# Mirrored odd heads, another order of grams and corner products, and gated weight splits in the chunk stage of a two-block model

## The reference

```python
proj = h @ w_in
pool_u, pool_g, q, k, v, ret_g, rw, rw_g, gate_logits = jnp.split(proj, points, axis=-1)
...
o_pool = causal_pool_mixer(pool_u, pool_w, pool_scale) * jax.nn.silu(pool_g)
...
def step(S, inp):
    r_t, w_t, k_t, v_t, a_t, b_t = inp
    sa = jnp.einsum('bhvk,bhk->bhv', S, a_t)
    S = (S * w_t[:, :, None, :] + sa[..., None] * b_t[:, :, None, :]
         + v_t[..., None] * k_t[:, :, None, :])
    return S, jnp.einsum('bhvk,bhk->bhv', S, r_t)

_, y = lax.scan(step, jnp.zeros((B, H, N, N), jnp.float32), xs)
```

## Time and profile before

| what | value |
|---|---|
| median of 3 runs | 1835.55 us (1833.15 to 1838.32) |
| the profiled execution | 1840.28 us, span 1838.2 us |
| granted PE clock, mean share of full speed | 0.968 |
| PE busy | 1718.2 us, 93% |
| PE weight loads busy | 1373.8 us, 75% |
| DVE busy | 1036.0 us, 56% |
| ACT busy | 800.7 us, 44% |
| POOL busy | 632.0 us, 34% |

### The profile page before, as it was taken

The page is one execution under the profiler, slowest core; times in us unless marked ns, Lnnn a source line. Parts: engine busy times, 40 slices in busy tenths (PEclk is TensorE's granted clock), DMA queues, the critical chain, the costliest instruction groups (busy, mean ns, idle before and its releaser), DMA issues. The chain is left out here.

```text
span 1838.2 us, 26011 instructions
## 1 busy us (share of the span) xinstructions
PE 1718.2 (93%) x10688; PEld 1373.8 (75%) x10688; DVE 1036.0 (56%) x1367; ACT 800.7 (44%) x1200; POOL 632.0 (34%) x344
## 2 busy tenths in 40 slices
PE   8999989999999899899999999989999999987783
PEld 6877778888888787688888888868888986544441
DVE  4346744666665325584556766443116627866675
ACT  2455522333223335542333222344337736866673
POOL 1336612424444434751243444433421021322210
PEclk7999989999999899998999999989999999999997
DMA  8223321215444323322122544333420067999994
GB/s 344 81 92 106 90 77 36 92 58 192 171 166 171 126 92 96 96 85 77 54 85 66 209 175 169 138 126 126 149 92 1 1 240 265 382 388 395 389 392 178
DMA packets 82605, 287.97 MB, mean 157 GB/s; under 512 B 30473, under 2 KB 30601, under 8 KB 65332
## 3 DMA queue, kind: packets, MB, share of 16 engines
q1 hardware_dynamic: 76708, 275.87, 41.6%
q0 software_dynamic: 5040, 8.25, 1.4%
q10 hardware_dynamic: 736, 2.14, 0.3%
HBM read 274.50 MB, written 22.61 MB: 162 GB/s over the span
## 5 line engine op out<-in xcount | busy, mean ns | idle before, releaser
L1525 POOL TENSOR_TENSOR wmem_r<-wmem,wmem_r 128x1024 fp32r<-128x1024 f32 x170 | 420.2, 2473 | 696.4 <-ACT wmem_r L1041 685.5
L721 PE MATMUL banks<-h_hi_r,wmem_r 128*128 128x512 f32 x1632 | 511.2, 392 | 6.9 <-POOL wmem_r L1525 6.9
L721 PEld LDWEIGHTS banks<-h_hi_r,wmem_r 128*128 128x128 f32 x1632 | 307.9, 189 | 77.0 <-POOL wmem_r L1525 9.4
L1041 ACT ACTIVATE wmem_r<-wmem 128x1024 fp32r<-128x1024 f32 x170 | 180.2, 1060 | 405.2 <-DMA wmem<-wstream 402.2
L721 PE MATMUL banks<-hT_r,wmem_r 128*128 128x512 f32 x816 | 319.0, 391 | 0.0
L721 PEld LDWEIGHTS banks<-hT_r,wmem_r 128*128 128x128 f32 x816 | 154.0, 189 | 31.3
L2725 DVE TENSOR_TENSOR slots_r<-slots,wmem_r 128x1024 fp32r<-128x1024 f32 x102 | 121.9, 1217 | 57.7 <-ACT wmem_r L2418 52.1
L2806 POOL TENSOR_TENSOR wmem_r<-wmem,wmem_r 128x1024 fp32r<-128x1024 f32 x30 | 74.8, 2493 | 202.3 <-ACT wmem_r L2276 202.3
L992 PE MATMUL banks<-slots_r,wmem_r 128*128 128x512 f32 x512 | 127.7, 389 | 0.0
L1465 DVE SCALAR_TENSOR_TENSOR ztp<-xT,c_act,ztp 128x256 f32<-128x256 f32 x168 | 122.8, 731 | 6.0
L741 PE MATMUL banks<-wmem_r,h_hi_r 128*128 128x512 f32 x384 | 118.9, 391 | 0.0
(11 more groups left out here) (450 smaller groups left out, 3043.1 us busy)
## 6 DMA issues: line engine op xcount, KB each, us to landing
wmem<-wstream SPq DMA_DIRECT2D x206, 512.0 KB, 3.3
slots<-experts SPq DMA_DIRECT2D x80, 1024.0 KB, 24.5
xT<-ada SPq DMA_DIRECT2D x24, 1024.0 KB, 5.8
xT<-experts SPq DMA_DIRECT2D x16, 1024.0 KB, 25.0
slots<-ada SPq DMA_DIRECT2D x8, 1024.0 KB, 18.0
x_keep<-xT SPq DMA_DIRECT2D x2, 2048.0 KB, 17.4
xT<-x_keep SPq DMA_DIRECT2D x2, 2048.0 KB, 8.1
dil_rows<-dil_once SPq DMA_DIRECT2D x1, 2560.0 KB
```

The lines of the kernel that those rows point to most:

```text
L721: mm = nc.tensor.matmul(o, r(lhs[:, k, :]), r(rhs[:, k, :]), start=(k == 0 and i == 0), stop=(k == KD - 1 and i == 2))
L1041: inc(nc.scalar.activation(r(chunk(b)[0]), w, ACT.Copy), "w_high")
L1525: inc(g.tensor_tensor(r(lo), lo, r(hi), ALU.subtract), "w_split")
```

## The change

Five things are changed, in both layers.

1. The list of jobs and PE's order: the diagonal grams come after the first gate projection instead of after the fourth, `bs` after the second, `tv` and `tb` after the third, and `tk` after the fourth. Only two of the first three grams stand ahead of the corner products; the third stands between `zp` and `zc`. ACT and SP follow this order, and ACT takes the three exponentials ahead of its copy of the first gate.
2. DVE takes all cumulative sums first, and the two products that need the key norms after them.
3. The sides depend on the head kind too: `v_side(m, e)` is `side_of[(m + e) % 2]`. In every product of a step the heads with `e` = 0 and `e` = 1 now use different halves of the partitions or of the output, and PE's loops take `e` inside `c`, so the two alternate. The transpositions are made by 64x64 pieces.
4. In a step ACT copies w of `e` = 0 and u of `e` = 1, and DVE copies w of `e` = 1 and u of `e` = 0. The last quarter of a gram is issued after the state's part of y, and the banks stand in another order.
5. POOL's splits in the chunk steps wait until the state of step 1, 3 or 5 is ready (`s_ready` 2, 4, 6), and its copies wait for an earlier split. The copies are made per head kind.

```diff
-        v_side = lambda m: side_of[m % 2]
-        u_side = lambda m: side_of[(m + 1) % 2]
+        v_side = lambda m, e: side_of[(m + e) % 2]
+        u_side = lambda m, e: side_of[(m + e + 1) % 2]
...
             project("pu")
-            project("pg")
-            after("rk_ready")
...
+            feature_job("pg0", FIRST["pg"])
             after("ar_ready", 1)
             after("bk_ready", 1)
             for x in range(NT // 2):
...
+            feature_job("pg1", FIRST["pg"] + 1)
+            after("rk_ready")
...
+            feature_job("pg2", FIRST["pg"] + 2)
...
+            for n in range(0, NT, 2):
+                token_rows("v", n, V_, v_side)
+            for n in range(0, NT, 2):
+                token_rows("b", n, A_, u_side)
+            feature_job("pg3", FIRST["pg"] + 3)
...
+            for m in range(GRAMS_FIRST - 1):
+                gram(m, gram_banks(m), range(CW))
             after("inv_spread")
             after("corner_ready")
             corner_products("zp", lambda at, i: zt[at, i, SUB:STEP], lambda at, i: tt[at, i, :], 1)
+            gram(GRAMS_FIRST - 1, gram_banks(GRAMS_FIRST - 1), range(CW))
             corner_products("zc", lambda at, i: tt[at, i, :], lambda at, i: zt[at, i, SUB:STEP], 0)
...
+                o_u = [open_bank(f"u{m}{e}") for e in range(2)]
+                more = m + GRAMS_FIRST < STEPS
+                if more:
+                    o_g = gram_banks(m + GRAMS_FIRST)
+                    gram(m + GRAMS_FIRST, o_g, range(CW - 1))
+
+                after("w_ready0", m + 1)
+                after("w_ready1", m + 1)
...
+                for c in range(CW):
+                    for e in range(2):
+                        mm = nc.tensor.matmul(o_u[e][u_side(m, e), heads[c]], zt[u_side(m, e), RW_H * (m // 2) + 2 * c + e, :],
...
+                if more:
+                    gram(m + GRAMS_FIRST, o_g, range(CW - 1, CW))
+                after("u_ready0", m + 1)
+                after("u_ready1", m + 1)
...
             for m in range(STEPS):
+                inc(v.tensor_copy(w_sb[u_side(m, 1), CW * RW_D:2 * CW * RW_D], bank(f"w{m}1")[u_side(m, 1), 0:CW * RW_D]), "w_ready1")
+                o = bank(f"u{m}0")[u_side(m, 0), 0:CW * RW_D].rearrange("p (c f) -> p c f", c=CW)
+                inc(v.tensor_copy(per_head(uv_of(m)[u_side(m, 0)])[:, 0], o), "u_ready0")
                 if m + GRAMS_FIRST < STEPS:
                     gram_mask(m + GRAMS_FIRST, 0)
...
+                after("v_copied", 2 * n + 2)
                 if n > 0:
+                    after("s_ready", 2 * n)
                     low(FIRST["retq"] + n - 1, FIRST["retq"] + n)
```

282 lines of the change are left out of this document (153 added, 129 removed).

## The result

The changed kernel takes 1823.62 us (median of 6 runs, 1819.75 to 1826.51) against 1837.09 us (6 runs, 1833.15 to 1839.87): ratio 0.9930, 95% interval 0.9918 to 0.9943. The gain is 13.5 us where 28.5 were forecast. The profiled execution took 1819.75 us, span 1818.0. Its stretches are those of the earlier trace rows, with two more for the grams and corner products: up to `rg`, `rg` to the first gram, grams and corner products, chunk steps, for each layer.

A forecast was written before the change was run, and what follows sets the result against it. PE was taken as the bound, busy 93% of the span, mostly with work in the chunk steps. 26.1 + 10.6 - 10.0 + 1.8 = 28.5 us gained, from a median of 1835.55 to 1807 us; range 1796 to 1825.

The forecast's parts named there:

- Step A: Chunk steps: w, y and u alternate halves, so periods fall from 5.70 to 4.35 or 4.0 us; 26.1 us gained.
- the row of s: Chunk steps: profile row where s alternates output halves and the next batch starts 0.52 us later; 0.55 taken for w, y.
- Without a gram ... they cost about 0.15 each: Steps 5 to 7, without a gram: the waits for the copies of w and u cost about 0.15 us each.
- I cost it at nothing: Chunk steps: POOL's gating of its three 2.4 us splits, due only when `retq` starts, was given no cost.
- Step B: Corner products: the waits for the inverse and the low clock go, 4.3 us taken per layer; 10.6 us gained.
- At full clock 256 records at the pace of the diagonal grams ... are 4.15 us: Corner products: 256 records 16 ns apart, the pace of 128 diagonal gram records in 2.10 us, take 4.15 us.
- With them I expect the low clock to go too: Corner products: with the waits of 2.63 and 1.87 us for the inverse, the half clock was to go.
- Step C: From the first gate to `rg`: a wait before the diagonal grams and half clock, 44.5 us per layer; 10.0 us lost.
- Step D: `rg`/`tg` projections: the waits of 0.82 and 1.01 us for splits of weights go; 1.8 us gained.
- the clock stays low: Rival, chance 0.14: small matmuls hold the clock down in the corner products and first step of each layer; 1816 us.
- the 10 us at 0.50: Sign of being wrong: a chunk stage that still has 10 us at half clock.
- PE starves before the diagonal grams: Rival, chance 0.07 (0.04 slower): POOL holds two products 4.4 us, half clock lasts; 10.4 us lost per layer, 1828 us.

The follow-up runs named there:

- control: The changed kernel once more, unedited: 1823.24 us, ratio 0.9927.
- spread2: Changed kernel, diagonal grams after the second gate, two ACT high parts later, v, b, k tokens each behind a projection, POOL's first `rg` split earlier: 1814.86 us.
- no_alternation: Changed kernel with the loops of w, u and y issuing all tiles of the first head kind before the second, mirrored layout kept: 1831.99 us.
- copies_undone: Changed kernel with both copies of w on ACT and both copies of u on DVE, as before: 1834.34 us.
- pool_ungated: Changed kernel without POOL's gates: its `retq` splits don't wait for the state, its copies of v not for splits: 1837.06 us.
- dummy32: Changed kernel with 32 more small matmuls in the wait before the diagonal grams: 1820.65 us.
- dummy64: Changed kernel with 64 more small matmuls in the wait before the diagonal grams: 1820.59 us.
- warm8: Changed kernel with seven matmuls of 128x512 in the wait before the diagonal grams: 1817.84 us.
- early_undone: Changed kernel with gates, bonus, diagonal grams and tokens again in the order of before: 1822.29 us.
- double_zc: Changed kernel with each matmul of the last corner products `zc` issued twice in a row: 1830.46 us.

## Why the prediction was wrong

The sum went into the right direction, and each mechanism was at work, but the gain is less than half. From the sums of squares to `retq` the two traces of the changed kernel (changed, control) are 18.0 and 15.6 us shorter than before, where 28.5 were summed.

*Step A, 26.1 forecast, 20.2 and 20.8 measured.* The mirrored halves overlap as the row of s said, and a step with a gram takes 4.24 us (4.35). Two terms failed. "Without a gram ... they cost about 0.15 each": PE waits 0.76 us for the copy of w and 0.27 for that of u, and the period is 4.35 instead of 4.0. The copy itself takes 0.42; the two hand-overs, PE to DVE and back, take the other 0.34, and I had counted 0.1. And step 0 up to s takes 4.44 and 4.64 us instead of 3.0. Its wait for ACT's last corner copies, 0.75 and 0.94 us, was in the sum with 0.6; what was not is the half clock, on which both layers start the steps (252.88 to 256.29, 833.15 to 839.98). spread2, whose second layer has the same wait and full clock, takes 3.68. Three periods by 0.35 and 1.44 for step 0, less four by 0.11, are 2.1 us: the first layer's 35.07 against 33.0. The second layer's 3.9 us over 33.0 are the same and the longer low clock: its first period is 5.32 us instead of 4.20.

*Its reading of the cause was too narrow.* Alternation alone gives 4.3 and 3.2 us per layer (no_alternation), the divided copies 5.5 and 4.7 (copies_undone), POOL's gate 7.6 and 6.7 (pool_ungated). These do not add, since each was measured with the other two in place. "I cost it at nothing" was wrong of the gate as a part of the change: the sum with a scaling of 0.46 us holds only because of it.

*Step B, 10.6 forecast, 6.2 and 3.0 measured.* The failed step is "At full clock 256 records at the pace of the diagonal grams ... are 4.15 us". The pace of 16 ns holds for 128 records, one block of instructions; here two and three quarter blocks stand in a row, and PE stops for the next one: 2.1 us in the first layer and 1.2 in the second before w of step 0 (control 2.2 and 1.7). That these are stops for instructions is shown by dummy32, dummy64 and warm8, which move them. A second step failed with it: "With them I expect the low clock to go too". The wait for the inverse went and the low clock did not. In the control it begins 3.1 and 4.7 us ahead of w of step 0, and that is the rest of what B lacks there, 1.4 and 2.3 us. What made the clock fall without that wait is not shown; the stops for instructions are the only idle time that the corner products have ahead of it. The windows of the earlier trace rows leave out a stretch: before the change the second layer had half clock too, through its corner products and into the steps.

```profile
838.48:848.72 10.24, 10.24 (x282) 10.06 (x276) 0.51 (x1) 5.46 (x10) 0.00 (x0) 0.50 0.26 100
```

Part of the stalls that I read in the trace of before as waits for other engines may be of this kind too. There PE starts again at 181.33 and 186.93 about 1.0 and 1.2 us behind the ends of such packets (180.34 and 185.71). That is argued from the times alone: copies of other engines end just ahead of both, and no run tells them apart.

*Step C, 10.0 forecast lost, 12.0 measured.* First gate and wait are 12.96 us (13.2 forecast, split otherwise: 5.74 and 7.22). The half clock was right in kind, and warm8 shows its cause. Not in the sum were the stops for instructions, 2.48 us in the first layer's tokens and 2.04 us before the second layer's fourth gate, where the sum had 0.9 for a bank. B and C belong together: the forecast had them nearly cancel (10.6 against 10.0), and early_undone bears that out: 7.6 us return before the first gram, 6.0 are lost at the corner products, and the time stays.

*Step D, 1.8 forecast, 2.4 measured.*

*The rest.* The gain was summed against one execution that lay 3.2 us above the median of six, and taken off the median. Traces show 15.6 and 18.0 us, medians 12.3 and 13.5. Which stretch of that execution was slow isn't settled.

Of the rivals, "the clock stays low" (1816) was right in part: in both layers the steps start at half clock, and the control has the 10 us at 0.50 that the prediction had named as a sign of being wrong. "PE starves before the diagonal grams" had the right place with 7.2 us instead of 9.2 (4.8 and 4.4), and no rival had the supply of instructions. The Trainium skill ("Runtime: NRT & Kernel Launch", Instruction fetch mechanics) states that instructions are read in blocks of 256 and that crossing into the next is mostly hidden. The trace agrees with the first part (16384 bytes a packet). For runs of small matmuls it does not agree with the second: where a crossing falls into such a run PE stops for 0.3 to 3.6 us. In the chunk steps, where the packets start 3.9 us or more apart, the second part holds and there is hardly a stop. By the 25 ns between starts of the Trainium skill ("TensorE: Matmul & The Clock Gate"), weighed in the prediction, double_zc would cost 3.2 us a layer, an estimate. It measured 2.9 to 3.6, so the time alone doesn't decide; the starts inside a block do, with 19 ns there and 16 ns in the diagonal grams.

## What to carry to other kernels

Count instructions, not only matmuls: where a stretch issues small matmuls faster than one block in 3.6 us, price it by blocks, and set large matmuls between blocks rather than joining bursts. A wait with "issue" as its releaser in the middle of a batch, behind the same record in every execution, is the sign; moving it with a few idle instructions proves it. At the first record of a batch the word proves nothing: the same "issue" stood there for a bank that ACT had to free, and a stop for instructions was put down to ACT. Compare with the end of the last copy and of the last packet.

When a change makes a loop's period shorter, look at every instruction of other engines that falls into it at a fixed phase. A split of 2.4 us that did little harm at one period cost 2.14 us in every second step at another, and a gate on the state was worth as much as the whole change.

Undo each part by itself before crediting one. Here the new order of the early part and of the corner products was worth nothing measurable, and undoing any one of three small parts of the steps cost more than half the gain.

## What was not expected of the hardware

- PE stops 0.3 to 3.6 us in a batch of small matmuls when the next 16384 bytes of instructions are late; asked for in a row, the packets start 3.3 to 3.9 us apart, each taking 0.9 to 1.5 us.
- After a wait of 7.2 us, 128 small matmuls took 3.3 to 3.7 us at a granted clock of 0.5 (1.2 GHz); after 1.2 us of wait behind 6.2 us of large matmuls, 2.10 us at 1.0 (2.4 GHz). With 3.95 us of small matmuls and then 3.3 us of wait they still took 3.5 us.
- Two batches of 8 matmuls that write different halves of the output overlap partly even when issued one behind the other: y and w take 1.43 us, against 1.96 on one half and 1.20 alternated.
